# Gates of the first 128 tokens: 128 indirect adding DMAs in place of 16 groups of one-hot matmuls

## The reference

```
    e1 = jnp.take_along_axis(i1, top_c // PEER_TOPK, axis=-1)
    e2 = jnp.take_along_axis(i2, top_c % PEER_TOPK, axis=-1)
    idx = e1 * N_KEYS + e2
    gates = jax.nn.softmax(top_v, axis=-1).astype(xn.dtype)
...
        act = jax.nn.gelu(jnp.einsum('phkd,pd->phk', u, xb), approximate=False)
        return jnp.einsum('phk,phkd->pd', gb * act, v_tab[ib])
```

## Time and profile before

| | |
|---|---|
| median of 3 runs | 1453.38 us (1451.49 to 1453.53) |
| profiled execution: span | 1451.0 us (first to last instruction; its own time is not given beside it) |
| PE busy | 1443.0 us, 99% |
| DVE, ACT, POOL busy | 1121.3 us (77%), 767.8 us (53%), 445.1 us (31%) |
| granted clock of PE | 1.000 |
| DMA queues used | SP's alone; POOL issues no DMA |
| stages of PEER (us of the span) | up tiles from 456.9; gate rounds 676.3 to 910.8; last 20 up tiles to 983.5; down tiles to the end |

### The profile page before, as it was taken

The page is one execution under the profiler, slowest core; times in us unless marked ns, Lnnn a source line. Parts: engine busy times, 40 slices in busy tenths (PEclk is TensorE's granted clock), DMA queues, the critical chain, the costliest instruction groups (busy, mean ns, idle before and its releaser), DMA issues.

```text
span 1451.0 us, 22297 instructions
## 1 busy us (share of the span) xinstructions
PE 1443.0 (99%) x7422; PEld 1202.6 (83%) x7422; DVE 1121.3 (77%) x1929; ACT 767.8 (53%) x1010; POOL 445.1 (31%) x208
## 2 busy tenths in 40 slices
PE   9999999999999999999999999999999999999999
PEld 8888887878788888888888888888888888888887
DVE  5979898876689999996999997355666666666665
ACT  7445787776645455555555555454444444444442
POOL 5867566347457778892000000000000000000000
PEclk9999999999999999999999999999999999999999
DMA  7544534457433666666888888979889888888883
GB/s 241 174 145 145 186 117 155 167 184 265 145 130 121 217 218 214 214 215 215 304 301 306 302 305 298 342 243 323 288 293 288 289 288 291 286 292 284 295 287 140
DMA packets 166708, 345.17 MB, mean 238 GB/s; under 512 B 13421, under 2 KB 78957, under 8 KB 164337
## 3 DMA queue, kind: packets, MB, share of 16 engines
q1 hardware_dynamic: 166640, 344.32, 70.3%
HBM read 268.76 MB, written 75.51 MB: 237 GB/s over the span
## 4 chain that ended last, share of the span: by engine, by line
PE 97%; ACT 1%; DVE 1%; DMA 0%; issue 0%; SPq 0%; ACTq 0%
PE ps L1293 32%; PE ps L1302 32%; PE ps L791 13%; PE ps L814 6%; PE ps L1331 4%; PE ps L1162 3%; PE ps L1001 1%; PE ps L1228 1%; PE ps L779 1%; PE ps L1011 1%; PE ps L1055 1%; PE ps L1235 1%; PE ps L863 1%; PE ps L839 0%; DMA xs<-in_x 0%
## 5 line engine op out<-in xcount | busy, mean ns | idle before, releaser
L1293 PE MATMUL ps<-hT_r,u_r 128*128 128x512 f32 x2048 | 470.3, 390 | 0.0
L1302 PE MATMUL ps<-v_r,w_pairs 128*128 128x512 f32 x2036 | 461.7, 389 | 0.0
L1293 PEld LDWEIGHTS ps<-hT_r,u_r 128*128 128x128 f32 x2048 | 382.8, 188 | 79.1
L1302 PEld LDWEIGHTS ps<-v_r,w_pairs 128*128 128x128 f32 x2036 | 382.1, 188 | 79.4
L2484 DVE TENSOR_TENSOR v_r<-vraw,v_r 128x1024 fp32r<-128x1024 f32 x128 | 156.8, 1225 | 147.3 <-ACT v_r L1804 147.3
L1804 ACT ACTIVATE v_r<-vraw 128x1024 fp32r<-128x1024 f32 x128 | 135.7, 1060 | 253.3 <-PE ps L1302 247.9
L506 POOL TENSOR_TENSOR w_r<-w_raw,w_r 128x1024 fp32r<-128x1024 f32 x85 | 222.6, 2625 | 150.7 <-ACT w_r L1410 104.9
L581 POOL TENSOR_TENSOR u_r<-uraw,u_r 128x1024 fp32r<-128x1024 f32 x60 | 173.3, 2901 | 41.8 <-ACT u_r L1731 41.7
L1750 ACT ACTIVATE act_stage<-ps 128x512 f32<-128x512 f32 x128 | 76.5, 598 | 181.3 <-PE ps L1293 181.2
L1731 ACT ACTIVATE u_r<-uraw 128x1024 fp32r<-128x1024 f32 x128 | 135.3, 1058 | 54.1 <-DMA uraw<-in_u 50.8
L1410 ACT ACTIVATE w_r<-w_raw 128x1024 fp32r<-128x1024 f32 x95 | 100.0, 1059 | 84.5 <-PE ps L814 33.1
(11 more groups left out here) (299 smaller groups left out, 1577.4 us busy)
## 6 DMA issues: line engine op xcount, KB each, us to landing
uraw<-in_u SPq DMA_DIRECT2D x128, 512.0 KB, 4.7
vraw<-in_v SPq DMA_DIRECT2D x128, 512.0 KB, 5.2
w_raw<-in_w SPq DMA_DIRECT2D x100, 512.0 KB, 3.5
acts_out<-act_stage SPq DMA_DIRECT2D x128, 256.0 KB, 2.3
gates<-stage SPq DMA_DIRECT2D x16, 2048.0 KB, 7.4
g_in<-gates SPq DMA_DIRECT2D x64, 512.0 KB, 6.6
act_in<-acts_out SPq DMA_DIRECT2D x128, 256.0 KB, 5.3
gates_pre<-pre_stage SPq DMA_DIRECT2D x24, 256.0 KB, 2.2
```

The lines of the kernel that those rows point to most:

```text
L1293: ins = pe.matmul(bank(s % 2), u2[s][:, w, k * P:(k + 1) * P], hr4[:, w, k, :], start=i == 0, stop=i == 15, skip_group_check=True)
L1302: ins = pe.matmul(bank(2 * q + h), w2[:, s, w, q * P:(q + 1) * P], v2[s][:, w, h * BANK:(h + 1) * BANK], start=start and w == 0, stop=stop ...
```

## The change

It handles the first 128 tokens (`N_SCAT` = 1 list of 128) without one-hots:

- Their part of `gates` is laid out as [e1, e2, token]. SP clears it with 32 DMAs of 256 KB out of a tile of zeros, one behind each of the first 32 up tiles.
- `finish_lists(0)` writes the weights to `place_of` and the cell's number, (e1 x 128 + e2) x 128 + token, to `place_at`: two more small instructions on DVE. Lists 0 are no longer transposed or taken.
- POOL, behind its 60 low parts, issues 128 indirect DMAs, each of 128 weights of 4 bytes (one per token), which add to their cells. It waits for the clearing and lists 0 first, and for all DMAs issued so far before each next head (7 times).
- Gate groups fall from 64 to 48, rounds from 16 to 12. The 12 up tiles of the four lost rounds stand ahead of the rounds (`N_TOP` = 72, `N_GATE` still 108). DVE makes the low parts from tile 60 on, as before (`POOL_LOWS`).
- A load of gates is one DMA of cells (128 rows of 2 KB) and one of rows (12 blocks). The first one of cells waits on SP, at the 8th of the last 20 up tiles (q = 7), until all adds have landed (`placed`).
- DVE's product of activation and gate is two instructions, of 128 and 384 columns.

```diff
-N_TOP, PER_BLOCK = 60, 12
-N_GATE = N_TOP + PER_BLOCK * (NBLK // 4)
+N_SCAT = 1
+POOL_LOWS = 60
+CLEARS = 32 * N_SCAT
+N_TOP, PER_BLOCK = 60 + 12 * N_SCAT, 12
+N_GATE = N_TOP + PER_BLOCK * (NBLK // 4 - N_SCAT)
...
+            pool.iota(token_col[:, :], pattern=[[1, 1]], base=0, channel_multiplier=1,
+                      allow_small_or_imprecise_dtypes=True).then_inc(const_made, 1)
+            pool.memset(zeros, 0.0).then_inc(const_made, 1)
...
+            pool.wait_ge(cells_cleared, 16 * CLEARS)
+            pool.wait_ge(list_ready, N_SCAT)
+            for h in range(PH):
+                at_least(pool, placed, 16 * h * TOPK * N_SCAT)
+                for c in range(h * TOPK, (h + 1) * TOPK):
+                    for t in range(N_SCAT):
+                        e = slice(t * P + c, t * P + c + 1)
+                        pool.indirect_dma_start(cells_dram.unsqueeze(1), bass.IndirectOffsetOnAxis(place_u[:, e], 0),
+                                                place_of[:, e], None, compute_op=ALU.add).then_inc(placed, 16)
...
+            sp.wait_ge(const_made, 6)
             for n in range(N_TOP):
                 load_u(n + 4, n % 4)
                 spill(n, n % 4)
+                if n < CLEARS:
+                    clear(n)
...
-                        sp.wait_ge(block_stored[s], 16 * NBLK // 2)
-                if q in (2, 4):
-                    part_of_g(0, 0, (q - 2) // 2 * NBLK // 2)
+                        sp.wait_ge(block_stored[s], 16 * ROW_BLOCKS // 2)
+                    rows_of_g(0, 0)
+                if q == 7:
+                    sp.wait_ge(placed, 16 * PH * TOPK * N_SCAT)
+                    cells_of_g(0, 0)
...
-                if n in TURN_AFTER:
+                if n in TURN_AFTER[N_SCAT:]:
                     turn_lists(TURN_AFTER.index(n))
...
-            four_hots(0, 0, lambda: low_u(N_TOP, N_TOP % 4), 3)
+            for n in range(POOL_LOWS, N_TOP - 6):
+                low_u(n, n % 4)
+            for g in range(4):
+                one_hots(g, g)
+                low_u(N_TOP - 6 + g, (N_TOP - 6 + g) % 4)
+            for n in range(N_TOP - 2, N_TOP + 1):
+                low_u(n, n % 4)
```

More of the change, by code:

```diff
@@ L247, in build @@
         iota_exp = carve("iota_exp", 17920, 128)
+        zeros = carve("zeros", 50192, 512)
+        place_at = carve("place_at", 51856, N_SCAT * P)
+        place_of = carve("place_of", 51984, N_SCAT * P)
         vraw = carve("vraw", 47104, 4096)
@@ L463, in wait_low_u @@
         def wait_low_u(eng, n):
-            if isinstance(n, int) and n < N_TOP:
+            if isinstance(n, int) and n < POOL_LOWS:
                 at_least(eng, u_lo, n + 1)
             else:
-                eng.wait_ge(u_lo_dve, n - (N_TOP - 1))
+                eng.wait_ge(u_lo_dve, n - (POOL_LOWS - 1))
         block = ctx.enter_context(nc.Block())
@@ L575, in _ @@
             pool.wait_ge(w_lo_ready, ITEMS - len(DVE_LOW))
+            pool.iota(token_col[:, :], pattern=[[1, 1]], base=0, channel_multiplier=1,
+                      allow_small_or_imprecise_dtypes=True).then_inc(const_made, 1)
+            pool.memset(zeros, 0.0).then_inc(const_made, 1)
             pool.iota(iota3, pattern=[[1, NKEYS], [0, PAIR]], base=0, channel_multiplier=0,
                       allow_small_or_imprecise_dtypes=True).then_inc(const_made, 1)
-            for n in range(N_TOP):
+            for n in range(POOL_LOWS):
                 pool.wait_ge(u_hi, n + 1)
@@ L689, in load_g @@
                 at_least(sp, w_full, (c - 1) * CH)
-                for b in range(0, NBLK, NBLK // 2):
-                    part_of_g(c, s, b)
+                cells_of_g(c, s)
+                rows_of_g(c, s)
             def load_act(n, s):
@@ L722, in gate_blocks @@
                     sp.wait_ge(gate_out, j * 16 + 4 * (b + 1))
-                    sp.dma_start(gates_dram[j * 4 + b], stage[:, b % 2 * NKEYS * BLK:(b % 2 + 1) * NKEYS * BLK]
+                    sp.dma_start(gates_dram[j * 4 + (4 * N_SCAT + b)], stage[:, b % 2 * NKEYS * BLK:(b % 2 + 1) * NKEYS * BLK]
                                  ).then_inc(block_stored[b % 2], 16)
@@ L728, in _ @@
             gate_blocks(0)
-            with sp.Fori(1, NBLK // 4) as j:
+            with sp.Fori(1, NBLK // 4 - N_SCAT) as j:
                 gate_blocks(j)
-            sp.wait_ge(gate_done, T // GT)
+            sp.wait_ge(gate_done, GROUPS)
             for n in range(N_GATE, NKEYS):
@@ L746, in _ @@
                         load_act(q // 3 - 1, q // 3 - 1)
-                elif q in (15, 17):
-                    part_of_g(1, 1, (q - 15) // 2 * NBLK // 2)
+                elif q == 15:
+                    cells_of_g(1, 1)
+                elif q == 17:
+                    rows_of_g(1, 1)
             def load_four(c, s):
@@ L1345, in _ @@
             gate_blocks(0)
-            with pe.Fori(1, NBLK // 4) as j:
+            with pe.Fori(1, NBLK // 4 - N_SCAT) as j:
                 gate_blocks(j)
@@ L1793, in _ @@
             act.wait_ge(list_ready, TT)
-            act.wait_ge(list_turned, TT)
+            act.wait_ge(list_turned, TT - N_SCAT)
             gate_blocks(0)
-            with act.Fori(1, NBLK // 4) as j:
+            with act.Fori(1, NBLK // 4 - N_SCAT) as j:
                 gate_blocks(j)
```

84 lines of the change are left out of this document (54 added, 30 removed).

## The result

| | median | runs |
|---|---|---|
| before | 1452.64 us | 4, 1451.49 to 1453.53 |
| changed | 1482.51 us | 4, 1472.96 to 1485.13 |

The changed kernel is slower: ratio 1.0192, 95% interval 1.0178 to 1.0206. The prediction (1438.1 us, 1435 to 1470) missed. The profiled execution's own time is 1485.13 us beside a span of 1483.4 us, against a span of 1451.0 before. The four times of the changed kernel spread over 12.2 us, those of the kernel before over 2.0.

A forecast was written before the change was run, and what follows sets the result against it. PE, busy 1443.0 of 1451.0 us, was taken as the bound; 15.3 us leave its program and all other terms cost 0, so 1453.4 - 15.3 = 1438.1 us, own range 1436 to 1442, full range 1435 to 1470.

The forecast's parts named there:

- The saving: On PE, four rounds lose their gate groups (15.1 us) and one transposition of lists goes (0.25 us): together 15.3 us.
- the price of the adds: On POOL, 128 issues of 1.4 us and eight landings of 2.3 us: 198 us, end at 864, cost 0.
- The landings: After each head's adds, eight landings of 2.3 us, as for the smallest common store; variant 7.4 us, end at 904.
- The bounds: Per add issue: lower 0.43 us from SP's own DMA, upper 2.40 us from POOL's pass over 128 x 1024 elements.
- The date: At the last up tiles, PE is hurt if the adds land later than about 930.
- the ring of up-tile weights: Four buffers; tile 120's load stands behind SP's wait at q = 7, with slack 6.3 us, some 3 with longer landing.
- Rival A: Late adds: SP stands at q = 7, the ring runs dry, PE waits; decides from 1.92 us per issue; chance 0.14.
- B, the crowding: Adds crowd the DMA engines above 47 ns per add, tile loads come late; 1456 at 64 ns; chance 0.12.
- C: POOL's adds hold DVE up in the rounds, from 0.18 us per add; 1471 to 1520 us; chance 0.10.
- D: Clearing not covered: in the first 32 up tiles the ring is late by over 4 us, 1442 to 1449; chance 0.04.
- the forecast's own 0 to 4: Cost of the 32 clearing stores behind the first 32 up tiles: taken as 0, with 4 us as the upper end.
- the case that each add pays the 2.0 us in turn: On POOL's adds, the skill page's fixed DMA cost paid one after another: 256 us, end at 922, 3 us before SP asks.

The follow-up runs named there:

- experiment 10: Changed kernel with clearing ahead of the up tiles, later reading of cells and earlier adds together, full computation: 1436.97 us, ratio 0.9891 to the kernel before.
- experiment 8: Changed kernel, but POOL issues the first two cell loads behind its last add, SP no longer waits, DVE and ACT prepare later: 1459.12 us, ratio 1.0049 to before.
- experiment 9: Changed kernel with POOL making 50 low parts and DVE the other ten, so adds start earlier: 1453.30 us, ratio 0.9997 to the kernel before.
- experiment 6: Changed kernel with stores of gates in the rounds cut from 2 MB to 128 KB: 1467.97 us, one run.
- experiment 5: Changed kernel with DVE's low parts computing 16 of 1024 columns from tile 60 on: 1471.01 us, one run.

## Why the prediction was wrong, point by point

**The saving was right.** -15.3 us were forecast; with every stop out of the way (experiment 10) the kernel is 15.5 us faster than before.

**The failed step is the price of the adds:** "I take the middle, 1.4 us: 128 x 1.4 + 8 x 2.3 = 198 us, the end at 864". Measured are 306 us and 976. Three parts were off. The issue itself, with the time to the next: 219.0 + 36.3 = 255.3 us in place of 179.2, which is 1.99 us each, above the 1.92 that I had named as the point of decision. The landings: 37.5 + 1.5 in place of 18.4; five of the seven waits were 6.3 to 8.2 us, and only two were under 2.3: 1.84 ahead of the rounds, and 1.62 at 942 us, while PE and SP stood. I had the 7.4 us of the big stores as a variant, but combined it only with the cheap issue. And 11.8 us of pauses, for which I had no term. The bounds (0.43 and 2.40 us) held; the middle between them had nothing to speak for it, and with both ends far apart I set the end of the adds 60 us ahead of their date on its strength. Against a late end I also set that the window was "nearly twice my estimate"; by my own numbers it was 264 us to 198, 1.3 times.

**The date was right, its path was not.** I had PE hurt if the adds landed after about 930. The measured date is 935.2, with PE running 4.3 us late, which is 930.9. But I let the ring of up-tile weights run dry at tile 120. In fact PE stopped one tile earlier, through the product on DVE and the order of ACT's program. I had asked what is queued behind the late data on SP alone; DVE and ACT wait for the same data, each with the up tiles' work behind it. Experiment 8 had to move their waits too. That the two paths give nearly the same date is luck.

**Rival A was the outcome, and its working comes near the measured time.** By its formula the end at 976 is (976 - 666 - 18) / 128 = 2.28 us per add, 46 us behind its 264, and 1438 + 46 = 1484; the profiled execution took 1485.13. So close a hit is in part luck: the stop is 40.9 us and not 46, and 6.6 us of other losses (the table: 2.0, 2.3, 2.3) make up for it. A had a chance of 0.14, and the upper end of 1470 cut off half of it, the half that came. Between prices of 0.43 and 2.40 us with the decision at 1.92, a quarter would have followed from the bounds alone. Its break-even, a stop of 15.3 us, was somewhat too high: the profiled executions of experiments 8 and 9, with stops of 15.17 and 14.35 us, took 1457.92 and 1455.56 us, 5.5 and 3.1 above the median before. Clearing and the slow clock behind a stop take some 2 us each.

**B, the crowding, did not slow PE in the rounds.** In the stretch 670 to 976 us queue q0 has 13.0% of 16 engines for 18432 packets, 306 x 16 x 0.13 / 18432 = 35 ns each, 39 ns per weight, under the 47 ns, and the rounds kept their 14.667 us. The crowding went the other way: the stores lengthened the waits for the adds (experiment 6).

**C had the contention right and the loser wrong.** DVE's one-hots still take 0.69 us and its low parts 1.22 us; it is POOL's adds that grow, from 1.54 to as much as 2.6 us. Single lines of DVE in the changed kernel:

```profile
L2493 DVE TENSOR_TENSOR onehots<-onehots,e_rows x48: 691/692/695, 692.2 to 880.6; 128x1024 bf16<-128x1024 bf16 x48
...
L2498 DVE TENSOR_TENSOR u_r<-uraw,u_r x68: 1216/1226/1282, 671.5 to 1006.7; 128x1024 fp32r<-128x1024 f32 x68
```

The Trainium skill's page "SBUF — State Buffer", under who interferes with whom, lets a DVE instruction with two SBUF inputs contend with a GpSimd instruction that reads SBUF. The traces agree: in experiment 5 the adds beside idle DVE take 1.54 to 1.56 us, those beside the bf16 one-hots, which have two SBUF inputs, up to 2.06, and in the changed kernel those beside the float32 low parts up to 2.57.

**D** did not happen: the up tiles lost 2.3 us beside the clearing, which is not its "over 4 us" but inside the forecast's own 0 to 4.

The Trainium skill's page "DMA: Bandwidth & Descriptors", in its section on the anatomy of one DMA on the GpSimd path, calls the generation of descriptors small and gives about 2.0 us per DMA, mostly completion. The trace shows the reverse for these adds: 1.54 us are spent on POOL, per instruction and one after another. The prediction's estimate for the case that each add pays the 2.0 us in turn, an end at 922, left 3 us of margin. It pointed the right way, and that it lies so near the measured 1.99 us per add is luck, for the mechanism is another.

## What to carry to other kernels

Price an operation that the trace lacks against its break-even, not by the middle of its bounds: where the break-even lies within them and nothing speaks for either end, the chance of failure is about the share of the range behind it. These small indirect DMAs were paid per instruction on the engine that issues them, so count instructions, and start them early or let their result be read late; the same adds cost 2% or bring 1.1% by their dates alone. When something comes late, follow its data through every in-order engine that consumes it: the first one to have other work queued behind it stops the kernel.

## What the runs showed of the hardware

- An indirect adding DMA of 128 weights of 4 bytes holds POOL for 1.54 us, one of 64 weights for 1.40, and 0.30 us pass to the next. Beside DVE's passes over 1024 columns with two inputs it takes up to 2.57 us (float32, changed kernel) or 2.06 us (bf16, experiment 5); DVE's own single instructions are at most some 0.05 us longer.
- POOL waited 1.6 to 9.5 us for the last add of a head before the next could start, 37.5 to 40.5 us in seven waits; with the stores of 2 MB cut to 128 KB it was 1.8 to 5.7 us, 24.5 in all. It was 1.62 us in the changed kernel while the DMA engines had nothing else to move.
- The 61st add of 128 weights was preceded by a pause of 2.65 to 8.74 us in all ten kernels with such adds, wherever it fell in time; with 64 weights per add the first pause came before the 114th. Why is open.
- PE restarted after a stop of 41 us at a granted clock of 0.53 for about 5 us, and after one of 15 us (experiment 8) at 0.55 for some 4.5 us: 2 us lost behind each stop.
